# Moving modulation work and sums between TensorE, VectorE, GpSimd and ScalarE in a four-layer fp32 kernel

## What is computed

```python
shift, scale, gate = split(silu(c) @ mod_w[i] + mod_b[i], 3)         # and the same from c_ctx
h_lat = rms_norm(x, g) * (1 + scale) + shift                          # and h_ctx
y_lat, y_ctx = mixer(h_lat, h_ctx)
x = x + gate * y_lat                                                  # and ctx, unless it is the last layer
```

## Time and profile before

| | us |
|---|---|
| median of 3 runs | 2879.95 |
| profiled execution | 2876.43 |
| its span | 2874.7 |
| TensorE busy | 2694.6 |
| VectorE busy | 1942.7 |
| ScalarE busy | 1217.1 |
| GpSimd busy | 314.5 |

### The profile page before, as it was taken

The page is one execution under the profiler, slowest core; times in us unless marked ns, Lnnn a source line. Parts: engine busy times, 40 slices in busy tenths (PEclk is TensorE's granted clock), DMA queues, the critical chain, the costliest instruction groups (busy, mean ns, idle before and its releaser), DMA issues.

```text
span 2874.7 us, 40435 instructions
## 1 busy us (share of the span) xinstructions
PE 2694.6 (94%) x13810; PEld 2159.6 (75%) x13810; DVE 1942.7 (68%) x2948; ACT 1217.1 (42%) x1861; POOL 314.5 (11%) x455
## 2 busy tenths in 40 slices
PE   5799999899799999999988999999998997999989
PEld 2477777687677777777777788888876876998878
DVE  4399999988746565655666666654454887875655
ACT  3255555522334344443444533333443314554643
POOL 1111011043100000000003200000000441110000
PEclk7799999999899999999999999999999998999999
DMA  8755455366455554545444355532221663883325
GB/s 357 294 184 168 157 171 181 127 224 218 141 191 181 188 188 175 194 170 190 175 175 149 117 182 161 161 119 92 74 73 38 227 205 109 295 281 111 124 92 172
DMA packets 121223, 490.97 MB, mean 171 GB/s; under 512 B 13872, under 2 KB 15920, under 8 KB 107824
## 3 DMA queue, kind: packets, MB, share of 16 engines
q1 hardware_dynamic: 74176, 267.49, 27.0%
q0 software_dynamic: 46960, 222.32, 22.8%
HBM read 487.66 MB, written 2.10 MB: 170 GB/s over the span
## 4 chain that ended last, share of the span: by engine, by line
PE 65%; DVE 20%; issue 7%; DMA 6%; ACT 2%; DVEq 1%; POOL 0%; ACTq 0%; POOLq 0%; SPq 0%
PE psum L246 15%; PE psum L248 15%; PE psum L247 15%; DVE w_lo L228 5%; DVE psum L376 4%; PE psum L259 4%; PE psum L296 3%; DVE work L378 2%; DMA work<-in_mod_units 2%; DMA y<-in_mod_weights 2%; PE psum L260 2%; PE psum L1509 1%; PE psum L1012 1%; PE psum L1050 1%; DVE work L890 1%
## 5 line engine op out<-in xcount | busy, mean ns | idle before, releaser
L246 PE MATMUL psum<-h_both,w_hi 128*128 128x512 f32 (+1 forms) x3264 | 1188.3, 364 | 15.7 <-DVE w_lo L228 15.6
L248 PE MATMUL psum<-h_both,w_lo 128*128 128x512 f32 (+1 forms) x3264 | 1158.6, 355 | 0.0
L247 PE MATMUL psum<-h_both,w_hi 128*128 128x512 f32 (+1 forms) x3264 | 1158.3, 355 | 0.0
L228 DVE TENSOR_TENSOR w_lo<-raw,w_hi 128x1024 fp32r<-128x1024 f32 x496 | 607.2, 1265 | 480.2 <-ACT w_hi L220 479.3
L246 PEld LDWEIGHTS psum<-h_both,w_hi 128*128 128x128 f32 x3264 | 620.9, 190 | 112.9 <-issue 15.4
L247 PEld LDWEIGHTS psum<-h_both,w_hi 128*128 128x128 f32 x3264 | 621.1, 190 | 93.5 <-issue 9.8
L248 PEld LDWEIGHTS psum<-h_both,w_lo 128*128 128x128 f32 x3264 | 620.3, 190 | 87.0
L220 ACT ACTIVATE w_hi<-raw 128x1024 fp32r<-128x1024 f32 x496 | 496.7, 1052 | 296.8 <-PE psum L248 207.0
L376 DVE SCALAR_TENSOR_TENSOR psum<-work,modraw 128x1024 f32<-128x1024 f32 x128 | 171.3, 1338 | 36.5 <-DMA work<-in_mod_units 36.0
L259 PE MATMUL psum<-h_both,w_hi 128*128 128x512 f32 x480 | 177.7, 410 | 15.6 <-DVE w_lo L228 8.6
L378 DVE SCALAR_TENSOR_TENSOR work<-work,modraw 128x1024 f32<-128x1024 f32 x128 | 158.6, 1239 | 0.0
(11 more groups left out here) (274 smaller groups left out, 3022.1 us busy)
## 6 DMA issues: line engine op xcount, KB each, us to landing
raw<-in_weights SPq DMA_DIRECT2D x496, 512.0 KB, 4.5
modraw<-in_mod_weights POOLq DMA_DIRECT2D x80, 1024.0 KB, 5.2
work<-in_mod_units POOLq DMA_DIRECT2D x128, 512.0 KB, 4.4
y<-in_mod_weights POOLq DMA_DIRECT2D x16, 1024.0 KB, 9.2
y<-in_mod_units POOLq DMA_DIRECT2D x32, 512.0 KB, 4.0
modraw<-in_mod_units POOLq DMA_DIRECT2D x32, 512.0 KB, 4.8
modraw<-in_cond_rows POOLq DMA_DIRECT2D x6, 1024.0 KB, 6.2
work<-in_gate_w POOLq DMA_DIRECT2D x16, 256.0 KB, 4.4
```

The source lines that it names most:

```text
L228: dve.tensor_tensor(w_lo[:, par, half, :], raw[:, 2 * par + half, :], w_hi[:, par, half, :].bitcast(F32), ALU.subtract).then_inc(S["split_ ...
L246: pe.matmul(dst, hi, h_hi[:, k, 0:n], start=(k == 0), stop=False)
L247: pe.matmul(dst, hi, h_lo[:, k, 0:n], start=False, stop=False)
L248: mm = pe.matmul(dst, lo, h_hi[:, k, 0:n], start=False, stop=(k == KT - 1))
```

## The change

Three things. First, GpSimd computes nothing any more in the out projections: VectorE adds the squares, one tile late, and x is no longer multiplied by its factor beforehand; the norm multiplies x with factor and root in one operation. Second, attention has 8 chunk groups instead of 16 (a chunk behind the K and the V strip only, one buffer), and VectorE makes 16 two-row and 16 one-row units there; their rows lie in `xl`, so x is stored in HBM meanwhile (`kept`) and read back. Units move: one from the LRU's last block to out projection 0, eight from out projection 2 to the SGU (3 per group). In the out projections units have two buffers (`mw_out`, in `y`). Third, the convolution's centre tap and bias are taken by ScalarE straight from PSUM. Besides, in out projection 1 the context rows are loaded after the last product with V instead of the last head's y, and the first squares stand behind the tanh of the rows; in attention's last rounds VectorE's weights stand ahead of the root; VectorE's and GpSimd's attention programs are written out whole, ScalarE's for 10 heads.

```diff
-MOD_GROUPS = M_ATT + HEADS1
+MOD_GROUPS = M_ATT + HEADS1 // 2
 def mod_load(pool, m, q):
-    pool.wait_ge(S["mod_used"], 4 * m + q - 1)
-    pool.dma_start(modraw[:, q % 2, :, :], ins["mod_weights"][4 * m + q]).then_inc(modraw_in[q % 2], 16)
+    pool.wait_ge(S["mod_used"], 4 * m + q)
+    pool.dma_start(modraw[:, 0, :, :], ins["mod_weights"][4 * m + q]).then_inc(modraw_in[0], 16)
...
+def unit_load_out(pool, p, halves=(0, 1)):
+    for half in halves:
+        if p not in (U_OUT0 - 1, U_OUT0, U_OUT2, U_OUT2 + 1):
+            pool.wait_ge(S["unit_used"], 2 * p + half - 3)
+        pool.dma_start(mw_out[:, p % 2, half, :], ins["mod_units"][2 * p + half]).then_inc(unit_sem[2 * (p % 2) + half], 16)
...
-HALVES = {0: (U_OUT0 - 1, [2, 1, 2, 2, 3, 2, 3, 2, 3, 3, 3, 2, 3, 3, 0, 0]),
-          2: (U_OUT2, [0, 0, 2, 3, 3, 2, 3, 3, 2, 3, 3, 2, 3, 3, 0, 0])}
+HALVES = {0: (U_OUT0 - 2, [2, 3, 2, 3, 2, 3, 2, 3, 2, 3, 3, 2, 3, 3, 0, 0]),
+          2: (U_OUT2, [0, 0, 2, 1, 2, 1, 2, 1, 2, 1, 2, 1, 1, 0, 0, 0])}
 def context(k, c):                                          # norm_dve
-    dve.tensor_tensor(hs4[c][:, 0:T], y[:, 0, k, :], nb["rstd"][:, 0:T], ALU.mult)
+    dve.scalar_tensor_tensor(out=hs4[c][:, 0:T], in0=xl[:, k, :], scalar=mod_a[:, bass.ds(k, 1), 0],
+                             in1=nb["rstd"][:, 0:T], op0=ALU.mult, op1=ALU.mult)
...
 # out_act, after the first two strips of layer 1
-if not near_end and l < 3:
+if l == 1 and isinstance(j, int) and j == 0:
+    if c == 0:
+        act.wait_ge(S["mod_cols"], MOD_GROUPS)
+    cb_tanh(act, C_SGU2, (2 * c, 2 * c + 1))
+    if c == 1:
+        squares(0, 0)
+        squares(0, 1)
+elif not near_end and l < 3:
     squares(j, c)
 # out_pool
-            pool.tensor_tensor(acc, acc, sqb[c], ALU.add).then_inc(S["sq_added"], 1)
-        pool.tensor_tensor(y[:, 0, m, :], xl[:, m, :], mod_a[:, bass.ds(m, 1), 0].to_broadcast([P, T]),
-                           ALU.mult).then_inc(S["xa_done"], 1)
 # out_dve
+    def add(m, c):
+        dve.wait_ge(S["sq_done"], KT * (l + 1) + m + 1)
...
+            dve.tensor_tensor(acc, acc, sqb[c], ALU.add).then_inc(S["sq_added"], 1)
...
 # lru_act, lru_dve
-act.activation(upad[:, :, 2:2 + T], two(psum[:, U_BANK, :]), ACT.Copy).then_inc(L["u_evac"], 1)
+act.activation(upad[:, :, 2:2 + T], two(psum[:, U_BANK, :]), ACT.Copy)
+ge(act, L["gate_done"], 4 * b)
+ge(act, L["bx_done"], 2 * b)
+act.activation(lw["xc"], psum[:, U_BANK, :], ACT.Identity, scale=col("conv_w", 4 * b + 2),
+               bias=col("conv_b", b)).then_inc(L["u_evac"], 1)
-step(dve.tensor_scalar(xc, upad[:, :, 0:T], col("conv_w", 4 * b), col("conv_b", b), ALU.mult, ALU.add))
-for w in range(1, CONV_W):
+for w in (0, 1, 3):
...
+    if not last:
         unit(dve, 2 * b, 0, GATE + b)
 # attention: halves of units at four places of each head
+ATT_UNITS = [0] + [4] * 8 + [0] + [6, 6, 6, 6, 4, 4]
+ATT_AT = {0: [0] * 4, 4: [1, 1, 1, 1], 6: [2, 2, 1, 1]}
...
+    pool.wait_ge(S["x_new"], KT)
+    pool.dma_start(kept, xl[:, :, :]).then_inc(S["x_kept"], 16)
...
+    for i in range(HEADS1):
+        if i == 9:
+            pool.wait_ge(S["unit_used"], 2 * U_GATE1)
+            cb_load(pool, C_GATE1)
+        chunk_in(2 * i + 1)
+        after(i, 0)
+        chunk_in(2 * i + 2)
+        for place in range(1, 4):
+            after(i, place)
...
+    pool.dma_start(xl[:, :, :], kept).then_inc(S["x_back"], 16)
 # att_dve: units(i, 0) after the split for strip 1, (i, 1) after that for strip 2, (i, 2) for strip 3, (i, 3) at the head's end
 # sgu_dve, layer 2: three units per group
-unit_half(dve, U_SGU2 + 2 * i + n // 2, n % 2, n // 2, 9 * KT + SCALE + 2 * i + n // 2, mw_y)
+for h in ((0, 1), (2,), (3, 4), (5,))[n]:
+    p = 3 * i + h // 2
+    unit_half(dve, U_SGU2 + p, h % 2, h // 2 % 2, 9 * KT + SHIFT + HALF + p, mw_y, unit_sem, IN_SGU2 + p + 1, lights=KT)
 # the Pool program
-pool.wait_ge(A["att_y"], HEADS1)
+pool.wait_ge(A["av"], HEADS1)
 pool.dma_start(y[:, 1, :, :], ins["ctx2_t"].rearrange("k p t -> p k t")).then_inc(S["ctx2_in"], 16)
```

More of the change, by code:

```diff
@@ L952, in rounds @@
                 body(i // 2, i % 2)
-            with eng.Fori(peel // 2, n // 2) as j:
-                for par in range(2):
-                    body(j, par)
+            if peel < n:
+                with eng.Fori(peel // 2, n // 2) as j:
+                    for par in range(2):
+                        body(j, par)
             for i in range(n, n + lag):
@@ L976, in att_strip, with att_halves @@
             return Strip(S_ATT, 4 * par + c, j, 8)
-        def att_pool(pool):
+        ATT_UNITS = [0] + [4] * 8 + [0] + [6, 6, 6, 6, 4, 4]
+        ATT_FROM = [2 * U_ATT + sum(ATT_UNITS[:i]) for i in range(HEADS1)]
+        ATT_AT = {0: [0] * 4, 4: [1, 1, 1, 1], 6: [2, 2, 1, 1]}
+        def att_halves(i, place):
+            if not isinstance(i, int) or i >= HEADS1:
+                return []
+            at = ATT_AT[ATT_UNITS[i]]
+            first = ATT_FROM[i] + sum(at[:place])
+            return [divmod(first + n, 2) for n in range(at[place])]
@@ L1134, in body, with units @@
                     act.activation(v_sb, psum[:, V_BANK, :], ACT.Copy).then_inc(A["v_sb"], 1)
-            rounds(act, body, HEADS1, 2, 4)
+                if isinstance(i, int) and i in (0, 9):
+                    cb_tanh(act, C_ATT if i == 0 else C_GATE1, range(4 if i == 0 else 2))
+            rounds(act, body, HEADS1, 2, 10)
         def att_dve(dve):
             kg = col("qk1", 1)
+            def units(i, place):
+                for p, half in att_halves(i, place):
+                    if p < U_GATE1:
+                        unit_half(dve, p, half, p % 2, 6 * KT + SHIFT + p - U_ATT, mw_y, unit_sem, IN_ATT + p - U_ATT + 1,
+                                  rows=rows_att, out=junk_att)
+                    else:
+                        unit_lat(dve, p, half, 3 * KT + GATE + p - U_GATE1, mw_att, rows_att[:, 0, :], IN_ATT + p - U_ATT + 1)
             def body(j, par):
@@ L1172, in body @@
+                if last:
+                    weights()
+                    root()
+                else:
+                    root()
+                    weights()
                 if last:
@@ L1245, in sgu_pool @@
             units(GROUPS - 2)
-            unit_load(pool, first + KT - 1, mw)
+            for n in range(1, per):
+                unit_load(pool, first + per * (GROUPS - 1) + n, mw)
         def sgu_pe(pe, lay):
```

286 lines of the change are left out of this document (171 added, 115 removed).

## The result

The changed kernel takes 2802.94 us (median of 4 runs, 2799.22 to 2805.79) against 2878.98 us for the kernel before (median of 4 runs, the three above among them): a ratio of 0.9732, 95% interval 0.9714 to 0.975. The profiled execution took 2805.79 us with a span of 2804.1 us, 70.6 us less than the span before. The forecast was 2803 us for the median and 74.6 us for the span.

A forecast was written before the change was run, and what follows sets the result against it. VectorE was taken to set the LRU's pace, TensorE attention's, with late VectorE work stretching out-projection strips. Terms summed to -74.6 us: 2801.8 from the profiled 2876.43, 2805 from the median 2879.95; forecast 2803, range 2786 to 2832.

The forecast's parts named there:

- The body: LRU blocks: one VectorE step of 0.69 us less in each of 14, 9.7 us saved, bounds 7 to 11.
- rival (c): LRU: the saving does not show because TensorE's own block time or ScalarE's added operation takes over; 2813 us, chance 0.07.
- The tail: LRU's last block: a whole unit of 4.96 us leaves VectorE; 4.3 us saved, bounds 0 and 8.
- Out projections 0 and 2: Stretched strips shrink towards 10.8 us as VectorE's load falls; 18 us saved in each, bounds 9 or 12 to 19.
- half the units are gone: Out projection 2: VectorE therefore has 3 us and more to spare per tile; 18 us saved.
- Attention: Two of four chunks per head go, turns come every second head: 1.39 us per head, 22.2 for 16, bounds 12 and 38.
- the turn into columns, 0.79, now comes every second head: Attention: halving these turns on TensorE was counted as 0.40 of the 1.39 us saved per head.
- (b): VectorE stays the bound in out projection 0 or attention: +12 to +16 us, 2817 us, chance 0.2.
- (d): Attention: VectorE's halves wait for their loads, so slower than before: +85 us, 2888 us, chance 0.03.
- Out projection 1: Rows loaded some 5 us earlier and squares behind both tanh pairs: 8.4 us saved, bounds 5 and 10.
- Norms: Three norms multiply x with two factors, 484 ns against 424, 16 times each: +3 us, 0 to 5.
- SGU of net 2: A third unit per group, 2.5 us of cover against a half of 2.3 plus waits: +2 us, 0 to 8.

The follow-up runs named there:

- e5_tap_on_vector: The changed kernel with VectorE making all four taps of the LRU's convolution again and ScalarE only copying: 2814.16 us.
- e6_halves_of_16: The changed kernel with each modulation half's two VectorE products made over 16 columns instead of 1024, loads and waits kept: 2775.48 us.
- e10_one_ahead_adds: The changed kernel with units of out projections 0 and 2 fetched one ahead and their squares added by GpSimd again: 2821.49 us.
- e1_units_2_16: The changed kernel with two units a group again in the SGU of net 2 and 16 in out projection 2: 2795.66 us.
- e4_gpsimd_adds: The changed kernel with GpSimd adding the squares again in out projections 0 and 2, the multiply of x not brought back: 2800.36 us.
- e7_ctx_late: The changed kernel with out projection 1's context rows loaded at the last head's y again, squares kept behind both tanh pairs: 2802.84 us.

## Why the prediction was right, and where its terms were off

**LRU.** The body gave 8.3 of the 9.7. Where VectorE sets the pace the step was costed rightly: blocks 5 to 15 gave 7.4 us, 0.67 each for the 0.69 written, and e5_tap_on_vector gives 0.65. The sum's mistake is the factor of 14: the first four blocks gave 0.9 us together, since they already stood near TensorE's own 25.22 us, as the lower bound had it. That floor (e6_halves_of_16) lies another 7.0 lower over the body, so rival (c) never came near. The tail gave 4.4 for 4.3: a unit out of VectorE's way, a shorter wait, and the square root next in line (VectorE waits 1.3 us for it now). No experiment undid the tail alone.

**Out projections 0 and 2.** 18.9 and 18.5 for 18 and 18, and the mechanism is the one written: VectorE's load against TensorE's 10.8 us a strip. The terms were about right in size too: 1.05 us of VectorE per operation of GpSimd (said 1.1), VectorE busy 142.98 us (said 147), and waits for landings of 19.9 us that went to none. In projection 2 the prediction named "half the units are gone" as the cause. That would have been enough (e10_one_ahead_adds), but so are the other two parts with all 16 units (e1_units_2_16). It had not asked whether the edit was needed, and so costed its price in the SGU as a fee for a gain that comes without it. What GpSimd's multiply of x cost by itself stays open.

On GpSimd and VectorE the Trainium skill (SBUF — State Buffer, the section on its two sides) says that a VectorE operation with two SBUF inputs and a GpSimd operation that reads SBUF lock each other out for as long as an operation lasts. Here an addition of 1.47 us (mean, e4_gpsimd_adds) cost VectorE 1.05: near it and below. That part of each addition falls beside such operations would explain the difference; no run here shows it.

**Attention.** The sum of the stage with its end was right (21.1 for 21.2), its parts were not. Per head the forecast of 1.39 came out as 1.22. The step that failed is "the turn into columns, 0.79, now comes every second head": it costs that when the rows are ready, and they were ready because of the chunk that the change takes away. The first two heads gave 5.1 where 2.4 had been written (two and a half of the 16 shares, less the microsecond for late loads): 3.6 of it is the strip behind head 0's gate, 14.83 us before and 11.24 after. There a chunk of 0.99 us went and a turn that waited 1.3 us for its rows besides its own 0.9, and the loads were not late. The second miss came out of taking one steady head for all. VectorE's extra halves cost nothing (e6_halves_of_16), as the walk through its order had it; rivals (b) and (d) did not come.

**Out projection 1.** 9.4 for 8.4, but by the other of the two edits: the order of the squares does it, and the earlier load adds at most 1.2, no more than the stage's scatter (e7_ctx_late).

**Norms.** 1.1 for 3, too small a difference to be settled beside their scatter. The multiply takes 481 ns where it took 424.

**SGU of net 2.** 7.7 for 2, at the upper bound; 6.1 without the first strip, which scatters. The step that failed is the cover: 2.5 us before TensorE's use were set against one more half of 2.3, and the waits of that half were left as "+ waits". They are most of it: VectorE waited 18.5 us for landings in the stage, and TensorE 4.1 us for what stood behind them. The rows had the sizes for it: a landing of 4.4 us from issue, one buffer per half, and two halves in a row where only one had been.

**The last SGU.** +4.0, of which 3.0 in one strip, was in no term. The other 1 us is the stage's first strip, 9.7 us here and 8.4 before; kernels with the changed kernel's code there show 8.4 as well. The change does not touch the stage, and nothing in the trace of before tells that a load there has no reserve except the load's own place in VectorE's order.

Over the whole table the misses on the dear side come to 14 us (the SGU 5.7, the last one 4.0, the steady heads 2.3, the LRU 1.3) and those on the other side to 10 (the first heads 2.7, the start, the norms and the kv stage 1.3 to 1.9 each, the projections 2.4). That the total agrees within 4 us is in part luck: misses of 14 and 10 us met. The two stages that hold half of the saving were right in size, projection 0 also by its mechanism, projection 2 with one cause named where each of two is enough.

## What to carry to other kernels

Add an engine's busy time, the stretch from its neighbours and its waits for landings, and set the sum against the pace of the engine that it feeds: well below that pace each of them is free, from about that pace on they are paid for: here one cost nothing, one 7.5 us when it brought the sum to the pace, and together they cost 16. Before work is moved to make room, try whether there is room once the other edits are in. Before a cost is multiplied by the number of rounds, look at the first rounds by themselves. When something is taken off the bound engine, ask what it covered: here 0.99 us of work hid 0.7 us of a copy, and putting that copy ahead of two operations gave 6.6 us back.

## What was not expected of the hardware

One load of 512 KB that GpSimd issues took 7.2 to 8.0 us to land in eleven kernels whose loads there are the same, where the median of such loads is 4.7, and the strip behind it took 7.9 to 10.9 us. In the kernel before it took 4.4 and with GpSimd's loop written out 5.3, and the strip 7.2 in both. The load that SP issues there, 0.3 us behind it, was slow as well (7.1 us in the changed kernel, 5.2 in the one before), so it is not GpSimd's load alone that is slow. The issue right before it comes more than a microsecond later than GpSimd's other ones of its kind in the kernel before too, where nothing follows from it. The cause stays open.

Behind one and the same wait the clock is lowered in some executions and not in others. The first LRU block holds a wait of TensorE of 3.0 or 3.1 us in all thirteen traces; it took 28.5 to 28.6 us at a mean granted clock of 1.00 in six of them and 30.3 us at 0.94 in seven. A stage with such a wait can differ by 1.7 us between traces without any difference in its code.
